# One head's v and its remainder as one stationary tile in an encoder's attention

## The reference

```
q = rmsnorm(cq @ w_uq), k = rmsnorm([ckv @ w_uk, k_rope])   8 heads of 96 dims, rotary on 32
v = ckv @ w_uv                                              8 heads of 64 dims
p = softmax(q k^T / sqrt(96))                               512 x 512 for each head
o = p v  -> 512 x 512;   branch_a = o @ w_attn_up           512 -> 1024
branch_b = glu(gelu(y) @ w_glu)                             y from the state-space branch
x = x + (gate_a * branch_a + gate_b * branch_b) @ w_o;  x = x + swiglu(rmsnorm(x))
```

## Time and profile before

| what | us |
|---|---|
| three runs | 1621.01, 1622.44, 1615.86; median 1621.01 |
| profiled execution, its own time | 1616.31 |
| its span | 1614.5 |
| PE busy in the span | 1550.9 (96%) |
| DVE busy | 884.8 (55%) |
| ACT busy | 591.3 (37%) |
| POOL busy | 557.8 (35%) |

### The profile page before, as it was taken

How to read it: one execution, slowest core, us unless ns; L and a number is a source line. 1 busy time by engine, 2 the same in 40 slices (tenths; PEclk the granted TensorE clock), 3 DMA queues, 4 the chain that set the end, 5 groups by cost and what they waited for, 6 DMA issues and landing times.

```text
span 1614.5 us, 21071 instructions
## 1 busy us (share of the span) xinstructions
PE 1550.9 (96%) x8352; PEld 1230.3 (76%) x8352; DVE 884.8 (55%) x1233; ACT 591.3 (37%) x992; POOL 557.8 (35%) x274
## 2 busy tenths in 40 slices
PE   8996998999999989999999899888999999999999
PEld 3554787778878877888888788777887888888887
DVE  5998477758547997558231862576684222112210
ACT  4561227653344231333331323676424223122220
POOL 0000013235434454434442333422434444434442
PEclk9998899999999999999999999999999999999999
DMA  7457720032232244453526362101422332322232
GB/s 253 157 173 258 277 88 1 1 105 91 92 120 91 79 148 155 147 160 91 169 96 246 117 231 89 50 1 40 118 79 91 105 104 82 101 91 95 88 104 79
DMA packets 73201, 188.34 MB, mean 117 GB/s; under 512 B 23568, under 2 KB 32144, under 8 KB 69008
## 3 DMA queue, kind: packets, MB, share of 16 engines
q1 hardware_dynamic: 43968, 145.18, 26.6%
q10 hardware_dynamic: 29136, 41.82, 8.0%
HBM read 154.47 MB, written 32.51 MB: 116 GB/s over the span
## 4 chain that ended last, share of the span: by engine, by line
PE 71%; DVE 15%; DVEq 5%; ACT 3%; DMA 2%; issue 2%; SPq 1%; POOL 0%; ACTq 0%; POOLq 0%
PE ps L1623 22%; PE ps L1624 22%; PE ps L1625 22%; PE ps L1767 2%; DVE qkTl L1479 1%; DVE nmx L1511 1%; DVE work L1036 1%; SPq L414 1%; ACT prob L945 1%; PE ps L1930 1%; DMA ctd_scr<-CPp 1%; PE ps L1921 1%; DVEq L1205 1%; DVEq L1163 1%; DVE work L1037 1%
## 5 line engine op out<-in xcount | busy, mean ns | idle before, releaser
L500 POOL TENSOR_TENSOR wl<-stage,wh 128x1024 fp32r<-128x1024 f32 x204 | 511.2, 2510 | 917.8 <-ACT wh L562 910.6
L562 ACT ACTIVATE wh<-stage 128x1024 fp32r<-128x1024 f32 x211 | 221.6, 1056 | 350.3 <-PE ps L1625 240.8
L1623 PE MATMUL ps<-xg2h,wh 128*128 128x512 f32 x704 | 280.7, 399 | 2.6 <-DVE act L1595 2.6
L1625 PE MATMUL ps<-xg2h,wl 128*128 128x512 f32 x704 | 279.1, 396 | 0.0
L1624 PE MATMUL ps<-xg2l,wh 128*128 128x512 f32 x704 | 279.0, 396 | 0.0
L1623 PEld LDWEIGHTS ps<-xg2h,wh 128*128 128x128 f32 x704 | 132.6, 188 | 35.5 <-issue 3.9
L1625 PEld LDWEIGHTS ps<-xg2h,wl 128*128 128x128 f32 x704 | 132.7, 188 | 32.2
L1624 PEld LDWEIGHTS ps<-xg2l,wh 128*128 128x128 f32 x704 | 132.8, 189 | 32.0 <-issue 0.5
L1623 PE MATMUL ps<-hidh,wh 128*128 128x512 f32 x352 | 139.8, 397 | 2.3 <-DVE hidl L1601 1.2
L1625 PE MATMUL ps<-hidh,wl 128*128 128x512 f32 x352 | 139.2, 396 | 0.0
L1624 PE MATMUL ps<-hidl,wh 128*128 128x512 f32 x352 | 139.2, 396 | 0.0
(11 more groups left out here) (271 smaller groups left out, 2840.4 us busy)
## 6 DMA issues: line engine op xcount, KB each, us to landing
stage<-in_stream SPq DMA_DIRECT2D x211, 512.0 KB, 3.2
CPTR<-ctd_scr ACTq DMA_DIRECT2D x6, 1664.0 KB, 10.3
slabs<-in_stream SPq DMA_DIRECT2D x16, 512.0 KB, 6.0
InT<-in_scr ACTq DMA_DIRECT2D x6, 1024.0 KB, 6.3
ctd_scr<-CPp SPq DMA_DIRECT2D x4, 1152.0 KB, 8.2
ctd_scr<-CPp ACTq DMA_DIRECT2D x4, 1152.0 KB, 6.6
in_scr<-BPI SPq DMA_DIRECT2D x4, 1024.0 KB, 5.1
in_scr<-BPI ACTq DMA_DIRECT2D x4, 1024.0 KB, 3.9
```

Of the source, the lines that this page charges most:

```text
L500: pool.tensor_tensor(wl[:, s, :], stage[:, (n - RAW) % STAGES, :], wh[:, s, :].bitcast(F32), ALU.subtract).then_inc(wl_ready, 1)
L562: return act.activation(o, i, ACT.Copy, **kw)
L1623: pe.matmul(o, wt[0], x[0], start=start, stop=False)
L1625: return pe.matmul(o, wt[1], x[0], start=False, stop=stop)
```

## The change

The tile `vv` replaces `vh` and `vl`. It holds, for each key tile, four blocks of 64 columns: the first head's high part, its remainder, the second head's remainder, its high part. A stationary side is the two blocks of one head, so that one pass makes the product with the high part in one half of the 128 output rows and the product with the remainder in the other half. Each key tile takes two matmuls (probabilities' high part, then their remainder) instead of three. The two halves must then be added: ACT copies the half with the remainder's product to the partitions of the other (`other`, tile `oth`), DVE adds it to the bank's other half (`added`), and one multiplication of the whole tile follows (`scaled`).

The products stand one unit later, in odd units. The steps behind them move: ACT copies `oth` in units 1 and 5, DVE adds in units 2 and 6, scales in unit 6 and makes `oTl` in unit 7, and ACT makes `oTh` in unit 7. The output projection's first nine matmuls stand between the last two products, and its first two slabs leave the last pair's part to the end.

```diff
-        vh = [r.take("vh0", [P, TT, P], F32R)]
-        vl = [r.take("vl0", [P, TT, P], F32R)]
+        vv = [r.take("vv0", [P, TT, 4, VD], F32R)]
+        oth = spare.take("oth", [P, SEQ])
@@ ACT
+                def other(hp, h):
+                    n = PAIRS * l + hp
+                    act.wait_ge(pv_done, 4 * n + 2 * h + 2)
+                    if hp:
+                        act.wait_ge(o_added, 2 * n - 1 + h)
...
+                    copy(oth[h * VD:(h + 1) * VD, :], ps[(1 - h) * VD:(2 - h) * VD, 4 + h, :]).then_inc(o_other, 1)
+                    if a >= UNITS and u == 1:
+                        other(hp - 1, 0)
                     if a >= UNITS and u == 2:
                         scales(hp - 1)
-                    if a >= UNITS and u == 4:
+                    if a >= UNITS and u == 5:
+                        other(hp - 1, 1)
+                    if a >= UNITS and u == 7:
                         output(hp - 1)
@@ DVE
+                def added(hp, h):
...
+                    dve.wait_ge(o_other, 2 * n + h + 1)
+                    tt(of[half, :], ps[half, 4 + h, :], oth[half, :], ADD).then_inc(o_added, 1)
+
                 def scaled(hp):
...
-                        tt(of[half, :], ps[half, 4 + h, :], Rn[half, :], MUL).then_inc(o_scaled, 1)
+                    dve.wait_ge(r_copied, PAIRS * l + hp + 1)
                     dve.drain()
+                    tt(of[:], of[:], Rn[:], MUL).then_inc(o_scaled, 1)
@@ PE
-                    if a >= 4 and a % 2 == 0:
-                        m = (a - 4) // 2
+                    if a == STEPS + 2:
...
+                        for k in range(PAIRS - 1):
+                            up_product(0, 0, k)
+                    if a >= 5 and a % 2:
+                        m = (a - 5) // 2
...
                         for t in range(TT):
-                            last = products(ps[:, 4 + h, tok], (vh[pair % 2][:, t, :], vl[pair % 2][:, t, :]),
-                                            (pTh[:, m % 2, t, :], pTl[:, m % 2, t, :]), t == 0, t == TT - 1)
+                            v = vv[pair % 2][:, t, 2 * h:2 * h + 2, :].rearrange("p a d -> p (a d)")
+                            pe.matmul(ps[:, 4 + h, tok], v, pTh[:, m % 2, t, :], start=(t == 0), stop=False)
+                            last = pe.matmul(ps[:, 4 + h, tok], v, pTl[:, m % 2, t, :], start=False, stop=(t == TT - 1))
                         last.then_inc(pv_done, 1)
+                for k in range(PAIRS - 1):
+                    up_product(0, 1, k)
+                ready(S_UP + 1)
+                pe.wait_ge(up_free, KT * l + 4)
+                for c in range(2):
+                    for k in range(PAIRS - 1):
+                        up_product(1, c, k)
+                for j in range(2):
+                    for c in range(2):
+                        last = up_product(j, c, PAIRS - 1)
+                    last.then_inc(slab_done, 1)
```

More of the change, by code:

```diff
@@ L63 @@
 UP_ORDER = [(c, k) for c in range(2) for k in range(PAIRS)]
-UP_FIRST = [(c, k) for c in range(2) for k in range(PAIRS - 1)] + [(c, PAIRS - 1) for c in range(2)]
 QKV = 2 * (QK + NOPE + VD)
@@ L336, in build @@
         r_copied = sem("r_copied")
+        o_other = sem("o_other")
+        o_added = sem("o_added")
         o_scaled = sem("o_scaled")
@@ L551, in _ @@
                             rotated()
-                        if u == 7:
-                            v_rest(hp + 1)
                     elif a < STEPS and u in (2, 4, 6):
                         remainder(SLABS * l + S_UP + u // 2 - 1)
+                    if a < STEPS and hp + 1 < PAIRS and u == 7:
+                        v_rest(hp + 1)
                 for n in range(S_UP + 3, SLABS):
@@ L889, in v_high @@
                         act.wait_ge(v_ready, PAIRS * l + 1)
-                    copy(vh[hp % 2][:], qkv[hp][:, :, QKC:QKV]).then_inc(vh_ready, 1)
+                    copy(vv[hp % 2][:, :, 0::3, :], qkv[hp][:, :, QKC:QKV].rearrange("p t (h q) -> p t h q", h=2))\
+                        .then_inc(vh_ready, 1)
                 def turned(hp, i):
@@ L901, in scales @@
                     if hp:
-                        act.wait_ge(o_scaled, 2 * n)
+                        act.wait_ge(o_scaled, n)
                     else:
@@ L1480, in turned @@
                         qkTh[hp % 2][:, c, :].bitcast(F32), MUL, SUB).then_inc(qkT_ready, 1)
-                def scaled(hp):
-                    n = PAIRS * l + hp
-                    dve.wait_ge(r_copied, n + 1)
-                    if hp:
-                        dve.wait_ge(oh_ready, n)
-                    for h in range(2):
-                        half = slice(h * VD, (h + 1) * VD)
-                        dve.wait_ge(pv_done, 4 * n + 2 * h + 2)
-                        tt(of[half, :], ps[half, 4 + h, :], Rn[half, :], MUL).then_inc(o_scaled, 1)
+                def added(hp, h):
+                    n = PAIRS * l + hp
+                    half = slice(h * VD, (h + 1) * VD)
+                    if hp:
+                        dve.wait_ge(o_ready, n)
+                    dve.wait_ge(o_other, 2 * n + h + 1)
+                    tt(of[half, :], ps[half, 4 + h, :], oth[half, :], ADD).then_inc(o_added, 1)
+                def scaled(hp):
+                    dve.wait_ge(r_copied, PAIRS * l + hp + 1)
                     dve.drain()
+                    tt(of[:], of[:], Rn[:], MUL).then_inc(o_scaled, 1)
                 def output(hp):
@@ L1511, in _ @@
                         dve.reduce_max(nmx[:, e:e + 1], ps[:, a % 2, :], AX.X, negate=True).then_inc(max_ready, 1)
+                    if a < STEPS and hp and u == 6:
+                        added(hp - 1, 1)
                     if a in (1, 2):
@@ L1530, in _ @@
                             turned(hp + 1, u - 3)
-                    if a >= UNITS and u == 3:
+                    if a >= UNITS and u == 2:
+                        added(hp - 1, 0)
+                    if a < STEPS and hp and u == 6:
                         scaled(hp - 1)
-                    if a >= UNITS and u == 4:
+                    if a < STEPS and hp and u == 7:
                         output(hp - 1)
+                added(PAIRS - 1, 0)
+                added(PAIRS - 1, 1)
                 scaled(PAIRS - 1)
@@ L1897, in _, with up_product @@
                 pe.wait_ge(qk_sqa, 8 * (l + 1))
-                for a in range(STEPS + 3):
+                def up_product(j, c, k):
+                    if j == 0:
+                        pe.wait_ge(o_ready, PAIRS * l + k + 1)
+                    return products(ps[:, 2 * j + c, :], weight(l, S_UP + j, k * 2 * P + c * P, P),
+                                    (oTh[:, k, :], oTl[:, k, :]), k == 0, k == PAIRS - 1)
+                for a in range(STEPS + 4):
                     hp, u = a // UNITS, a % UNITS
@@ L1939, in _ @@
                         if pair and m % 2 == 0:
-                            pe.wait_ge(o_scaled, 2 * (PAIRS * l + pair - 1) + h + 1)
+                            pe.wait_ge(o_added, 2 * (PAIRS * l + pair - 1) + h + 1)
                         pe.wait_ge(pT_ready, STEPS * l + 2 * m + 2)
                         for t in range(TT):
-                            last = products(ps[:, 4 + h, tok], (vh[pair % 2][:, t, :], vl[pair % 2][:, t, :]),
-                                            (pTh[:, m % 2, t, :], pTl[:, m % 2, t, :]), t == 0, t == TT - 1)
+                            v = vv[pair % 2][:, t, 2 * h:2 * h + 2, :].rearrange("p a d -> p (a d)")
+                            pe.matmul(ps[:, 4 + h, tok], v, pTh[:, m % 2, t, :], start=(t == 0), stop=False)
+                            last = pe.matmul(ps[:, 4 + h, tok], v, pTl[:, m % 2, t, :], start=False, stop=(t == TT - 1))
                         last.then_inc(pv_done, 1)
-                for j in range(4):
+                for k in range(PAIRS - 1):
[9 more added lines that the diff above has]
+                    last.then_inc(slab_done, 1)
+                for j in range(2, 4):
                     ready(S_UP + j)
                     pe.wait_ge(up_free, KT * l + 2 * j + 2)
-                    for c, k in UP_FIRST if j == 0 else UP_ORDER:
-                        if j == 0 and c == 0:
-                            pe.wait_ge(o_ready, PAIRS * l + k + 1)
+                    for c, k in UP_ORDER:
                         last = products(ps[:, 2 * (j % 2) + c, :], weight(l, S_UP + j, k * 2 * P + c * P, P),
```

17 lines of the change are left out of this document (12 added, 5 removed).

## The result

| | before | after |
|---|---|---|
| median (lowest to highest), us | 1618.43 (1614.63 to 1622.44), 4 runs | 1641.56 (1637.71 to 1653.43), 4 runs |
| ratio | | 1.0151, 95% interval [1.0121, 1.0181] |
| profiled execution, own time, us | 1616.31 | 1642.06 |

A forecast was written before the change was run, and what follows sets the result against it. No engine was taken as full; order and waits between engines bound the kernel. 2 x 0.6 - 4 x 0.4 + 0.9 + 1.8 = 2.3 us gained, from 1618.7 to 1616.4, given as 1616; range 1603 to 1625.

The forecast's parts named there:

- the clock: Rival: gaps before the attention's reciprocals lower TensorE to 1.2 GHz for some 4 us each; 12 us in all, 1628; 6%.
- The first rival: Attention pairs: VectorE's wait at unit 7 is absorbed, TensorE sets the pace, 17.5 us a pair; 1595 us; 14%.
- The GELU: After the last pair: oTl and the loads come 1.6 us later; 0.9 us of stall in layer 1, none in layer 2.
- the nine projection matmuls between the products: End of the last pair: they change nothing in its 18.3 us sum, only fill the time in which pTl is made.
- no slack at all: Layer 1 before: the last gyl ended at 367.64 and the GLU's product needing it stood at 367.7.
- The test named for this: Sign that the forecast is wrong: a GLU that waits for gyl by more than 2 us.
- The last pair: From its scores behind the reciprocals to the projection: 18.3 us against 20.1, a gain of 1.8 us.
- The middle pairs: Between spread reciprocals: 21.45 us against 21.05, 0.4 us lost each; the reciprocal, 2.2 us early before, becomes late.
- The clash: Middle pairs: oTl meets POOL's remainder of v on the shared ports and waits 0.75 us.
- The first pair: Start of each attention, without oTh and oTl yet: the next scores start earlier, a gain of 0.6 us in each layer.

The follow-up runs named there:

- e1: Changed kernel with unread matmuls filling TensorE's gaps in the third and fourth pair and behind them; 1627.51 us, 1.0074 of before.
- e3: Changed kernel with the scaling moved to the next pair's unit 0 and the output (oTh, oTl) to its unit 1; 1630.62 us, 1.0075 of before.
- e7: Changed kernel with scaling and output in the next pair's units 0 and 1, and the last two products where they stood before; 1614.32 us, 0.9969 of before.
- e8: Kernel before with products a unit later, each head scaled by itself in units 3 and 4, output in unit 5; 1632.01 us, 1.0088 of before.
- e12: As e7, with the last pair's weight slabs split in units 4, 6 and 7 instead of 1, 3 and 5; 1619.33 us, 0.9991 of before.
- e4: Changed kernel with the products of probabilities and v in even units again, ACT and VectorE steps left as changed; 1630.16 us, 1.0079 of before.
- e9: Changed kernel with products in even units and the last two where they stood, no projection matmul between; 1617.69 us, 1.0009 of before.
- e11: Changed kernel with the last products where they stood before and TensorE's gaps filled with unread matmuls; 1624.24 us, 1.0047 of before.
- e10: As e9, with the scaling in the next pair's unit 0 and the output in its unit 1; 1619.42 us, 1.0020 of before.
- e2: Changed kernel with only VectorE's output step oTl moved behind the reciprocal of the next pair's unit 0; 1631.25 us, 1.0078 of before.

## Why the prediction was wrong

**The step that failed is the clock.** The sum took every TensorE duration at full clock, and the slower rival, "the clock", had 6% and 12 us. It was the case. Measured: 4.9 and 4.7 us in the attentions (after against e1) and about 1.65 us in each GLU, some 13 us in all. That the rival's 12 us come close is in part luck: it had 2 us in each of six pairs, and the attentions have 9.6 us in all and the GLUs the rest. The 25.8 us of the profiled executions are then 12.9 for the clock, 6.0 for the waits in the GLUs, 1.1 for the attentions at full clock (e1 against before, which has a lowered clock of its own in layer 1), and 5.8 outside the stages. The fault was in how the rival was weighed. I set the mean share of a pair, 77%, beside the share of a stretch of ten us, and did not look at where the idle time lies. The first rival says that the chain holds TensorE "for some 4 us before the reciprocals", and 2.61 + 1.74 = 4.35 came. The clock's rival counts only "a gap of over 2 us before the reciprocals". The larger part lies ahead of the scores of unit 1, which wait for the exponential of unit 7 behind the scaling and the maximum. The place mattered too: the product was moved behind the reciprocals, so that both run at 1.2 GHz and on the path.

**The GELU was mis-sized.** 0.9 us of stall in layer 1 and none in layer 2 were taken; the longest wait is 2.31 and 2.30 us, all waits for gyl cost 2.8 and 3.2, and with the clock behind them it is 4.5 and 4.8. The step "the nine projection matmuls between the products change nothing in this sum, they only fill the time in which pTl is made" is wrong: they hold the last product, and with it oTl and the loads, while the GLU's start does not move with them. For layer 1 "no slack at all" was right. Of the 3.2 us by which the GLU's start comes nearer to oTl (20.1 to 16.9) 0.3 were taken back (22.2 to 21.9). In layer 2 the slack that was taken was there, about 1.5 us, but the last gyl ends 22.1 us behind oTl and not 20.7: the high part beside POOL's slab took what was left. The test named for this, a wait for gyl of more than 2 us, is what came.

**The last pair lost a term.** 18.3 us against 20.1 were both counted from the scores behind the reciprocals. But in the changed kernel these scores stand a product, 0.95 us, further behind the reciprocals. The chain of the middle pair has this term, the last pair's did not. At full clock (e1) the stretch from the third reciprocals to the GLU is 44.4 us against 44.1 before: nothing gained where 1.8 was forecast. The lost term is 0.95 of these 2.2 us; the rest is not taken apart.

**The middle pairs.** Right: oTl waits 1.29 us for oTh ("about 1.3"), lasts 1.35 ("over 1"), the releaser is prc, pTl's wait is gone, oth takes 0.59 (0.60 taken). The distance is 0.5 us over the forecast even at full clock, and most of this is there before the scaling: it starts at 16.6 us in the pair (296.19 - 279.55), the chain has 16.2 (17.5 less 0.60 and 0.69). The clash was well sized: oTl lasts 0.66 us longer than at 355.22, and 0.75 was taken. POOL's instruction ended at 298.89 + 1.28 = 300.17, and oTl 0.55 us later, at 300.72. The Trainium skill (SBUF — State Buffer, section "SBUF: two separate sides") has VectorE blocked until the GpSimd instruction that holds the ports is done; the trace agrees.

**The first pair.** From the attention's first score to the first reciprocals it is 22.0 us after in both layers, and 24.3 and 23.2 before. The gain in layer 2 is 1.2 us where 0.6 was taken. In layer 1 before had a lowered clock in its first ten us, which the 2.3 us there contain.

**The rivals.** "TensorE sets the pace" was wrong for this kernel. With scaling and output elsewhere, e3 and e7 come to 19.4 and 19.7 us in the middle pairs at full clock, and not to 17.5. "A unit later" was not free by itself, which no rival held (e8).

Open: why the same gap is followed by a lower clock in one pair and not in the next (1.82 us in e7 and e12, 2.62 in e4 and e9); why e1, e3, e9, e11 and e12 spread by 14 to 18 us over their runs and e7 by 6, where e1 and e11 have their gaps filled, so that these gaps are not the reason for all; why the lowered clock outside the stages differs from one profiled execution to the next; and why e10 is not faster than before, when both its attentions are and its profiled execution lost 10 us outside the stages.

## What to carry to other kernels

Before taking matmuls off an engine that is nearly full, write down where its idle time will lie: here waits of 2.6 and 1.7 us in a pair were followed by half the clock for the work behind, and the loss is largest where that work is on the path. The length of a wait alone did not tell whether the clock would fall. So shorten the waits or put work into them (here small steps moved behind the reciprocals, or the product ahead of them), and price the slow case by the rows at the lower clock. And where a consumer two stages on has no slack, follow each instruction that is put ahead of its producer down to it.

## What the runs showed of the hardware

- Unread matmuls in TensorE's gaps made the kernel faster, 1.0151 to 1.0074 of before; in the last three pairs of the first layer the granted clock was 1.00 instead of 0.88, and sixteen small matmuls took 1.58 us instead of 2.88.
- The clock fell behind a single gap too: 2.14 us in e7, 2.31 in the GLU, and 1.82 in e12, where e7 had passed 1.82 us four times at full clock. A gap of 2.6 us passed at full clock once each in e2, e4 and e9 and was followed by a fall elsewhere in the same executions.
- The 64x512 copy from a bank to other partitions took 593 ns, the 128x512 copy 595 ns: half the partitions saved nothing.
- A 128x512 cast on VectorE with one SBUF input took 0.41 us alone and 2.58 us beside POOL's remainder of a slab (374.50 in the changed kernel).
